# Dilated attention rewritten as one run of sixteen steps, with scores issued two steps ahead

## The reference, cut to what matters

```python
DIL_GROUPS = ((128, 1), (512, 4), (2048, 16))
...
def dilated_mixture(q, k, v):
...
    for gi, (window, dilation) in enumerate(DIL_GROUPS):
        hs = slice(gi * HEADS_PER_GROUP, (gi + 1) * HEADS_PER_GROUP)
        o, l = dilated_attention(q[:, :, hs], k[:, :, hs], v[:, :, hs], window, dilation, slopes[hs])
        outs.append(o)
        lses.append(l)
    wts = jax.nn.softmax(jnp.stack(lses, axis=0), axis=0)
    y = jnp.sum(wts[..., None] * jnp.stack(outs, axis=0), axis=0)
```

## Time and profile before

| what | before |
| --- | --- |
| median of 3 runs | 3152.41 us (3146.73 to 3152.45) |
| profiled execution, its own time | 3146.47 us |
| its span | 3144.6 us |
| TensorE busy | 2830.1 us (90%) |
| DVE, ACT, POOL busy | 1629.2 us (52%), 649.0 us (21%), 178.0 us (6%) |
| mean granted clock of TensorE | 0.941 of full |
| the stage, from its first scores to the last copy's start | 2123.8 to 2297.1 us of the span |

### The profile page before, as it was taken

How to read it: one execution, slowest core, us unless ns; L and a number is a source line. 1 busy time by engine, 2 the same in 40 slices (tenths; PEclk the granted TensorE clock), 3 DMA queues, 4 the chain that set the end, 5 groups by cost and what they waited for, 6 DMA issues and landing times.

```text
span 3144.6 us, 44003 instructions
## 1 busy us (share of the span) xinstructions
PE 2830.1 (90%) x17517; PEld 2057.1 (65%) x17517; DVE 1629.2 (52%) x2182; ACT 649.0 (21%) x1101; POOL 178.0 (6%) x203
## 2 busy tenths in 40 slices
PE   5799668899989989999799999979889988889998
PEld 3455443688878868888355655565567776668886
DVE  6677672544445554444455555542355463365554
ACT  3133311211011021110222222222221121121101
POOL 2000110000000000000111110000000000000000
PEclk8899768999999999999899999999789989999999
DMA  7376201333332323333111111112023332223332
GB/s 229 116 238 198 70 0 47 89 91 100 92 88 87 94 80 93 94 94 95 49 30 30 31 30 31 32 55 66 24 59 93 87 85 62 60 75 98 96 93 67
DMA packets 404222, 255.33 MB, mean 81 GB/s; under 512 B 19880, under 2 KB 389121, under 8 KB 403969
## 3 DMA queue, kind: packets, MB, share of 16 engines
q1 hardware_dynamic: 400496, 243.63, 26.6%
q0 software_dynamic: 2320, 5.11, 0.5%
q10 hardware_dynamic: 1280, 4.78, 0.4%
HBM read 250.60 MB, written 2.10 MB: 80 GB/s over the span
## 4 chain that ended last, share of the span: by engine, by line
PE 84%; DVE 9%; issue 3%; ACT 3%; DMA 1%; DVEq 0%; ACTq 0%; POOL 0%; SPq 0%; POOLq 0%
PE PS L722 13%; PE PS L723 13%; PE PS L724 13%; PE PS L1398 5%; PE PS L709 4%; PE PS L737 3%; PE PS L738 3%; PE PS L739 3%; PE PS L1373 3%; PE PS L1150 3%; PE PS L1461 1%; PE PS L1379 1%; PE PS L1487 1%; PE PS L1583 1%; PE PS L1485 1%
## 5 line engine op out<-in xcount | busy, mean ns | idle before, releaser
L748 DVE CAST WH<-W 128x1024 fp32r<-128x1024 f32 x304 | 210.9, 694 | 719.0 <-PE PS L724 547.8
L750 DVE TENSOR_TENSOR WL<-W,WH 128x1024 fp32r<-128x1024 f32 x304 | 372.5, 1225 | 10.4
L723 PE MATMUL PS<-XNL,WH 128*128 128x512 f32 x864 | 342.8, 397 | 0.0
L722 PE MATMUL PS<-XNH,WH 128*128 128x512 f32 x704 | 277.1, 394 | 0.0
L724 PE MATMUL PS<-XNH,WL 128*128 128x512 f32 x704 | 275.3, 391 | 0.0
L724 PE MATMUL PS<-HH,WL 128*128 128x512 f32 x672 | 261.5, 389 | 0.0
L722 PE MATMUL PS<-HH,WH 128*128 128x512 f32 x672 | 261.5, 389 | 0.0
L723 PE MATMUL PS<-HL,WH 128*128 128x512 f32 x672 | 261.5, 389 | 0.0
L737 PE MATMUL PS<-XNH,WH 128*128 128x512 f32 x448 | 180.3, 402 | 32.6 <-DVE XNL L681 32.5
L738 PE MATMUL PS<-XNL,WH 128*128 128x512 f32 x480 | 193.9, 404 | 0.0
L1398 PE MATMUL PS<-HXF,W 128*128 128x512 f32 x336 | 167.5, 625 | 22.4 <-DVE ARENA L2549 11.5
(11 more groups left out here) (467 smaller groups left out, 4812.9 us busy)
## 6 DMA issues: line engine op xcount, KB each, us to landing
ARENA<-in_ada_w SPq DMA_DIRECT2D x80, 512.0 KB, 5.1
W<-in_ffn_w SPq DMA_DIRECT2D x64, 512.0 KB, 3.9
W<-in_w_in SPq DMA_DIRECT2D x51, 512.0 KB, 4.1
W<-in_ffn_w_gate SPq DMA_DIRECT2D x44, 512.0 KB, 3.8
W<-in_ffn_w_up SPq DMA_DIRECT2D x44, 512.0 KB, 3.7
W<-in_ffn_w_down SPq DMA_DIRECT2D x32, 512.0 KB, 3.8
W<-in_sc_w_in SPq DMA_DIRECT2D x24, 512.0 KB, 3.7
W<-in_ada_w SPq DMA_DIRECT2D x16, 512.0 KB, 4.9
```

The costliest lines, as they stand in the source:

```text
L722: nc.tensor.matmul(dst, WH[:, h, c], hi(k), start=(start and k == 0), stop=False)
L723: nc.tensor.matmul(dst, WH[:, h, c], lo(k), start=False, stop=False)
L748: nc.vector.tensor_copy(WH[:, h, :], W[:, s, 0:D]).then_inc(parted, 1)
L750: nc.vector.tensor_tensor(WL[:, h, :], W[:, s, 0:D], WH[:, h, :], ALU.subtract).then_inc(freed[s], 1)
```

## The change

The two passes of eight steps become one run of sixteen steps `n` on all three engines. Scores of step n+2 are issued ahead of the transposes of step n (before: n+1, and none across the border of the halves). DVE does `b` and `max` of step n+1 ahead of `inv` and `p` of step n, and ACT does `exp` of step n+1 ahead of the copies of step n. `SD` gets a third buffer. `DIL_FILL` says in which step a unit is filled: units 1 to 5 stay in steps 0 to 4, and units 6, 7 and 8, the values of the second half, go to steps 6, 8 and 10. The row maxima and sums move out of the arena into tiles of their own, the memory tokens move further down in the arena, and the progress of both halves is counted on one semaphore an engine.

```diff
+DIL_STEPS = 16
+DIL_FILL = {0: 1, 1: 2, 2: 3, 3: 4, 4: 5, 6: 6, 8: 7, 10: 8}
...
+        NEGMAX2, ROWSUM2 = sb("NEGMAX2", 8), sb("ROWSUM2", 8)
...
+        dil_steps = lambda names: " ".join(names(n) for n in range(DIL_STEPS))
+        dil_turns = lambda n: " ".join(f"t{n}{g}" for g in range(NG))
+        dl_pe = prog("dl_pe", "s0 s1 " + dil_steps(lambda n: (f"s{n + 2} " if n + 2 < DIL_STEPS else "") + (f"pv{n // 4 - 1} " if n and n % 4 == 0 else "")
+                                                   + dil_turns(n)) + " pv3")
+        dl_act = prog("dl_act", "exp0 u0 " + dil_steps(lambda n: (f"exp{n + 1} " if n + 1 < DIL_STEPS else "") + ("o0 " if n == 8 else "") + dil_turns(n)
+                                                       + (f" u{DIL_FILL[n]}" if n in DIL_FILL else "")) + " o1")
+        dl_dve = prog("dl_dve", "b0 max0 " + dil_steps(lambda n: (f"b{n + 1} max{n + 1} " if n + 1 < DIL_STEPS else "") + f"inv{n} p{n}"))
...
-        YA, DBIAS, SD, PTD, DIL1 = t_dl(2, T), t_dl(2, NG, T), t_dl(2, NG, T), t_dl(NG, NT, T), t_dl(DIL_UNITS, T)
-        NEGMAX2, ROWSUM2 = t_dl(8), t_dl(8)
+        YA, DBIAS, SD, PTD, DIL1 = t_dl(2, T), t_dl(2, NG, T), t_dl(3, NG, T), t_dl(NG, NT, T), t_dl(DIL_UNITS, T)
...
+            def scores(n):
+                half, e, qt = n // 8, n // 4 % 2, n % 4
+                own = DIL[half]
+                if n:
+                    pe.wait_ge(dl_dve.sem, dl_dve.done(f"b{n - 1}"))
+                if n == 8:
+                    pe.wait_ge(dl_act.sem, dl_act.done(f"u{2 * NG - 1}"))
+                for g in range(NG):
+                    mm = nc.tensor.matmul(bank[g][:, 0:(qt + 1) * P], own[halves[e], g, qt * P:(qt + 1) * P], own[halves[e], NG + g, 0:(qt + 1) * P], start=True, stop=True)
+                mm.then_inc(dl_pe.sem, dl_pe.step(f"s{n}"))
+            def turn(n, g):
+                if g == 0:
+                    pe.wait_ge(dl_dve.sem, dl_dve.done(f"p{n}"))
+                if n:
+                    pe.wait_ge(dl_act.sem, dl_act.done(f"t{n - 1}{g}"))
+                for c in range(n % 4 + 1):
+                    mm = nc.tensor.transpose(bank[DL_TURN[g]][:, c * P:(c + 1) * P], SD[:, n % 3, g, c * P:(c + 1) * P], IDENT)
+                mm.then_inc(dl_pe.sem, dl_pe.step(f"t{n}{g}"))
+            def values(n):
+                half, e = divmod(n, 2)
+                pe.wait_ge(dl_act.sem, dl_act.done(f"t{4 * n + 3}{NG - 1}"))
+                if half:
+                    pe.wait_ge(dl_act.sem, dl_act.done("o0"))
...
-                scores(0)
-                fill(0, range(KD))
-                for s in range(8):
-                    if s < 7:
-                        scores(s + 1)
-                    if s == 4:
-                        values(0)
-                    fill(s + 1, range(0, 3))
-                    for g in range(NG):
-                        turn(s, g)
-                        fill(s + 1, (range(3, 5), range(5, 7), range(7, KD))[g])
-                values(1)
-            dilated_attention(0)
-            pe.wait_ge(dl_act[0].sem, dl_act[0].done(f"u{DIL_UNITS - 1}"))
-            dilated_attention(1)
...
+            scores(0)
+            fill(0, range(KD))
+            scores(1)
+            for n in range(DIL_STEPS):
+                if n + 2 < DIL_STEPS:
+                    scores(n + 2)
+                if n and n % 4 == 0:
+                    values(n // 4 - 1)
+                if n in DIL_FILL:
+                    fill(DIL_FILL[n], range(0, 3))
+                for g in range(NG):
+                    turn(n, g)
+                    if n in DIL_FILL:
+                        fill(DIL_FILL[n], (range(3, 5), range(5, 7), range(7, KD))[g])
+            values(3)
...
+            def exps(n):
+                at, w = n % 8, (n % 4 + 1) * P
+                act.wait_ge(dl_dve.sem, dl_dve.done(f"max{n}"))
+                nc.scalar.activation(SD[:, n % 3, :, 0:w], SD[:, n % 3, :, 0:w], ACT.Exp, bias=NEGMAX2[:, at:at + 1],
+                                                 accum_out=ROWSUM2[:, at:at + 1]).then_inc(dl_act.sem, dl_act.step(f"exp{n}"))
+            def head_pair(half):
+                act.wait_ge(dl_pe.sem, dl_pe.done(f"pv{2 * half + 1}"))
+                nc.scalar.activation(YA[:, half, :], bank[5], ACT.Copy).then_inc(dl_act.sem, dl_act.step(f"o{half}"))
+            exps(0)
+            filled(0)
+            for n in range(DIL_STEPS):
+                if n + 1 < DIL_STEPS:
+                    exps(n + 1)
+                if n == 8:
+                    head_pair(0)
+                qt = n % 4
+                for g in range(NG):
+                    if n and qt == 0 and g == 0:
+                        act.wait_ge(dl_pe.sem, dl_pe.done(f"pv{n // 4 - 1}"))
+                    act.wait_ge(dl_pe.sem, dl_pe.done(f"t{n}{g}"))
+                    nc.scalar.activation(PTD[:, g, 0:qt + 1, qt * P:(qt + 1) * P],
+                                                     bank[DL_TURN[g]][:, 0:(qt + 1) * P].rearrange("p (c t) -> p c t", t=P), ACT.Copy).then_inc(dl_act.sem, dl_act.step(f"t{n}{g}"))
+                if n in DIL_FILL:
+                    filled(DIL_FILL[n])
+            head_pair(1)
...
+            own = lambda n: SD[:, n % 3, :, 0:(n % 4 + 1) * P]
...
+                if n >= 3:
+                    dve.wait_ge(dl_pe.sem, dl_pe.done(f"t{n - 3}{NG - 1}"))
...
-                biased(0)
-                for s in range(8):
-                    dve.wait_ge(dl_dve[half].sem, dl_dve[half].done(f"b{s}"))
-                    nc.vector.tensor_reduce(NEGMAX2[:, s:s + 1], own(s), AXXY, ALU.max, negate=True).then_inc(dl_dve[half].sem, dl_dve[half].step(f"max{s}"))
-                    if s < 7:
-                        biased(s + 1)
-                    dve.wait_ge(dl_act[half].sem, dl_act[half].done(f"exp{s}"))
-                    nc.vector.reciprocal(ROWSUM2[:, s:s + 1], ROWSUM2[:, s:s + 1]).then_inc(dl_dve[half].sem, dl_dve[half].step(f"inv{s}"))
-                    dve.wait_ge(dl_dve[half].sem, dl_dve[half].done(f"inv{s}"))
-                    ts(own(s), own(s), ROWSUM2[:, s:s + 1], None, ALU.mult).then_inc(dl_dve[half].sem, dl_dve[half].step(f"p{s}"))
+            biased(0)
+            row_max(0)
+            for n in range(DIL_STEPS):
+                if n + 1 < DIL_STEPS:
+                    biased(n + 1)
+                    row_max(n + 1)
+                total = ROWSUM2[:, n % 8:n % 8 + 1]
+                dve.wait_ge(dl_act.sem, dl_act.done(f"exp{n}"))
+                nc.vector.reciprocal(total, total).then_inc(dl_dve.sem, dl_dve.step(f"inv{n}"))
+                dve.wait_ge(dl_dve.sem, dl_dve.done(f"inv{n}"))
+                ts(own(n), own(n), total, None, ALU.mult).then_inc(dl_dve.sem, dl_dve.step(f"p{n}"))
```

More of the change, by code:

```diff
@@ new lines, in turn @@
+            def turn(n, g):
[11 more added lines that the diff above has]
+                    pe.wait_ge(dl_act.sem, dl_act.done("o0"))
+                    pe.wait_ge(dl_act.sem, dl_act.done(f"u{DIL_UNITS - 1}"))
+                for c in range(NT):
+                    for g in range(NG):
+                        mm = nc.tensor.matmul(bank[5][halves[e], c * P:T], DIL[half][:, 2 * NG + g, c * P + e * HEAD:c * P + (e + 1) * HEAD], PTD[:, g, c, c * P:T],
+                                              start=(c == 0 and g == 0), stop=(c == NT - 1 and g == NG - 1))
+                mm.then_inc(dl_pe.sem, dl_pe.step(f"pv{n}"))
@@ new lines, in fill @@
+            def fill(u, ks):
+                s = ring.slot("dil", u)
+                if ks[0] == 0:
+                    if u:
+                        pe.wait_ge(dl_act.sem, dl_act.done(f"u{u - 1}"))
+                    pe.wait_ge(landed[s], ring.arrived("dil", u))
+                for k in ks:
+                    mm = dilated_product(u, k, tiles(s)[:, k, :]) if u < 6 else dilated_tokens(k, lambda n: tiles(s)[:, n, :])
+                if ks[-1] == KD - 1:
+                    mm.then_inc(freed[s], 1)
@@ L1638, in _ @@
+            values(3)
             pe.wait_ge(mem_in, 16)
-            pe.wait_ge(dl_act[1].sem, dl_act[1].done("o"))
+            pe.wait_ge(dl_act.sem, dl_act.done("o1"))
             for m in range(4):
@@ L2020, in _ @@
             act.wait_ge(rz_dve.sem, rz_dve.done("out"))
[L2021 to L2028, removed]
-                for s in range(8):
[L2030 to L2035, removed]
-                        if qt == 0 and g == 0:
-                            if e:
-                                act.wait_ge(dl_pe[half].sem, dl_pe[half].done("pv0"))
-                            elif half:
-                                act.wait_ge(dl_pe[0].sem, dl_pe[0].done("pv1"))
-                        act.wait_ge(dl_pe[half].sem, dl_pe[half].done(f"t{s}{g}"))
-                        nc.scalar.activation(PTD[:, g, 0:qt + 1, qt * P:(qt + 1) * P],
-                                                         bank[DL_TURN[g]][:, 0:n].rearrange("p (c t) -> p c t", t=P), ACT.Copy).then_inc(dl_act[half].sem, dl_act[half].step(f"t{s}{g}"))
```

(25 more changed lines are left out.)

65 lines of the change are left out of this document (2 added, 63 removed).

## The result

The changed kernel takes 3126.14 us at the median of five runs (3119.22 to 3127.92), the kernel before 3152.41 (3142.56 to 3157.60, five runs now): a ratio of 0.9915, with a 95% interval from 0.9896 to 0.9933. The profiled execution has a span of 3123.6 us against 3144.6.

The account below looks back on a forecast made before the run. TensorE and DVE taking turns in the second half, with the clock falling, was taken as the bound. Stage: 101.5 + 36.0 + 8.1 + 4.2 = 149.8 us against 173.3; 3152.4 - 23.5 = 3129 us, range 3117 to 3139.

Parts of the forecast that it names:

- What bounds: Second half of the stage: TensorE and DVE take turns, neither is the bound; TensorE busy 51.82 of 70.70 us, clock 0.66.
- The two terms for work: TensorE in the stage: 101.5 us for first half and all nine units, 36.0 for the second half at full clock.
- Waits that the new order leaves: TensorE's remaining waits: 1.1 us at steps 2, 8 and 12, 4.1 at step 14, 0.7 before the last value products; 8.1 us.
- The clock: Tail: clock falls at the 4.1 us wait, costing 1.0, 1.3 and 1.9 us in transposes and last value products, 4.2 us.
- I charge nothing for them: The three 1.1 us waits, alone among dense work, cost no clock fall: an earlier window busy 3.92 of 5 us kept 1.00.
- The rival of falls at short waits: Clock also falls at the three 1.1 us waits, about 1.9 us a fall: gain 17 us, time 3135, chance 0.15.
- The rule on short idles: Skill text: short idles between matmul groups cycling through PSUM banks swing the clock; by it, falls at short waits were likelier.
- The third buffer: SD's third buffer removes a wait that would else bind: b of step n+2 would need the transposes of step n.
- Costs taken as nothing: Merge weight transfers, bias transfer, copies delayed by exp, third buffer and moved small tiles were all taken to add no time.
- The slower rival: Clock falls at step 6 and stays at 1.2 GHz to the end: stage about 216 us, time 3195, chance 0.04.
- The base: The 23.5 us gain was taken off the 3152.4 us median, which lay 5.9 us above the profiled execution.

Follow-up runs that it names:

- e7: Changed kernel with unit 0 split around step 1's scores, last head widest first, units 6 to 8 in steps 5, 9, 10: 3114.21 us, ratio 0.9892.
- e5: Changed kernel with the last two steps of unit 0 placed behind the scores of step 1: 3113.40 us, one run.
- e6: Changed kernel with the last head's query blocks in reverse order, widest first: 3121.59 us, one run.
- e4: Changed kernel with two score buffers instead of three: 3137.93 us, one run.
- e1: Changed kernel's unit placement in one run of sixteen steps, but scores one ahead, old DVE and ACT order, two buffers: 3155.89 us, ratio 1.0033 to the kernel before.
- e8: Changed kernel with scores one step ahead on TensorE, new DVE and ACT order kept: 3156.44 us, one run.
- e10: The changed kernel unaltered, run and profiled again: 3123.80 us, ratio 0.9917 to the kernel before.

## Why the prediction was right

The forecast was 3129 us, from 3117 to 3139; measured were 3126.14. The stage was forecast at 149.8 us and took 148.2.

- *What bounds.* Right. The two engines took turns, and the clock followed. In the table the 25.0 us between the two stages are 12.0 of idle time and 13.0 of slow work: the clock's share was at least that of the waits removed. The two terms for work came to 137.5 us (101.5 and 36.0), where e7, with the same low clock at the stage's start, measured 136.8. The lower bound of the second half's 36.0 should read 35.7, not 35.5.
- *Waits that the new order leaves.* Forecast 8.1 us: 1.1 three times, 4.1 and 0.7. Measured 7.8: 3.1 for the three, 4.0 and 0.7, each at its place. The transposes of steps 5 to 13 waited for nothing.
- *The clock.* The sum was close (4.2 forecast, 3.9 measured), but by luck: two misses of nearly the same size cancelled. In the tail the fall cost 4.76 us for 21 transposes against the 2.7 of my terms, 2.1, and the value products 0.1 instead of 1.9, since the clock had risen again by 2268. The step that failed was "I charge nothing for them": behind the wait ahead of the scores of step 2 the clock fell, 4.30 instead of 2.77 and 2.32 instead of 2.13 us, 1.7 together, and e5, without the wait, had no such fall. The ground given for that step was a misreading: the clock had not come through the idle time of the window from 2225 to 2230 unharmed, since the next window of the earlier trace rows is the fall itself, 0.58. The rival of falls at short waits was true at one place of three, at a price (1.7 us) near the 1.9 that it gave a fall.
- *The rule on short idles.* What the Trainium skill says (TensorE: Matmul & The Clock Gate, "A second HAM failure mode: psum-queue depth-cycling"), that short idles between groups of matmuls can make the clock swing, these traces bear out in part: behind a wait of 1.05 us the clock fell at step 2 in four executions of seven, among them both of the changed kernel, and in e6 behind one of 1.0 us at step 8, while the waits of 1.0 us at 2199 and 2232 of the changed kernel went by at 1.00.
- *The third buffer.* Priced at nothing with the note that without it a wait would bind: e4 measured 14 us.
- *Costs taken as nothing.* The part behind the stage took 848.4 us, 0.9 more than before; between 847.6 and 848.9 in the experiments, and 851.8 in e1. Beyond this 0.9 us nothing gained in the stage was given back there.
- *The slower rival* did not occur in this kernel. e1 and e8 showed a part of its mechanism: the first pieces of units slowed along with the rest (4.94 and 4.24 us in e1, 4.87 and 5.21 in e8, where 2.87 is full rate). But the clock rose again within each of these units and did not stay low to the end.
- *The base.* The gain of 23.5 us was taken off the median, not off the profiled execution. The medians differ by 26.3 us in these runs and by 25.0 in those of e10, so the choice served; how far it was luck can't be told from five runs each.
- *Not foreseen:* the stage began at 2117.0 to 2131.7 us in the kernels of this study, with the same code ahead of it. That is why single times order the kernels less well than the stage does.

## What to carry to other kernels

Where two engines hand work to and fro through one PSUM bank set and a few buffers, count the lookahead on every engine and every buffer. One run with scores two ahead gained 25 us of the stage with three buffers and 11 with two; one run by itself gave 4.5 to 7 of them, and reordering DVE without scores two ahead made the stage 13 us longer. Fill work protects the clock only where it closes the waits. Put between waits that stay, as in e1, part of it runs at the lower clock itself. In a chain of steps of unequal width let the last ones be the narrow ones: in e6 that shortened the stage by 3.9 us.

## What the runs showed of the hardware

A wait of 1.05 us in otherwise dense work was enough for the granted clock to fall from 1.00 to a mean of 0.69 over the 4 us from 2140 on, and waits of about the same length some 60 and 94 us later were not. Which of them does it could not be read from the length of the wait: with the same work and the same wait at step 2 it fell in four executions and held in three, and in those four it had risen earlier at the start of the stage. Without the wait (e5 and e7) it held. In the tail it was back soon: 0.52 from 2264 to 2268, a window with 3.77 of 4 us busy, and 1.00 in the window from 2268 on, in which the 0.7 us wait of the last value products ends.
